# Second block, attention: the relative bias comes from a skewed table and is added to the mask on GpSimd, not by a matmul on TensorE

## The reference, cut to what matters

```
q, k, v, qi, ki, wi = jnp.split(h @ w_in, A_SPLITS, axis=-1)
score = jnp.einsum('bth,bths->bts', wib, relu(qi . ki * IDX_DIM ** -0.5))
score = jnp.where(causal, score, -jnp.inf)
_, idx = lax.top_k(score, top_k)                  # top_k = 64
bias = rel_table[rel_bucket(q_pos - idx)]         # one value per head and distance
logits = q . k[idx] * scale + bias
p = jax.nn.softmax(jnp.where(valid, logits, -jnp.inf), axis=-1)
o = p @ v[idx];   out = o @ w_out
```

## Time and profile before

| | |
|---|---|
| median of 3 runs | 1785.63 us (1784.55 to 1786.57) |
| the profiled execution, its own time | 1787.35 us |
| its span in the profile | 1785.6 us |
| TensorE busy | 1611.1 us, 90% |
| VectorE, ScalarE, GpSimd busy | 898.4, 722.1, 168.2 us |
| mean granted TensorE clock | 0.946 of full speed |

### The profile page before, as it was taken

The page is one execution under the profiler, slowest core; times in us unless marked ns, Lnnn a source line. Parts: engine busy times, 40 slices in busy tenths (PEclk is TensorE's granted clock), DMA queues, the critical chain, the costliest instruction groups (busy, mean ns, idle before and its releaser), DMA issues.

```text
span 1785.6 us, 26627 instructions
## 1 busy us (share of the span) xinstructions
PE 1611.1 (90%) x11038; PEld 1328.8 (74%) x11038; DVE 898.4 (50%) x1104; ACT 722.1 (40%) x936; POOL 168.2 (9%) x82
## 2 busy tenths in 40 slices
PE   6999985767676689999998999999999999999998
PEld 4877742323232358999997999989999899998886
DVE  4765210101010158566585765686656657566665
ACT  4434220101010155445335544464445665355443
POOL 0200000000000002111001111111111001111110
PEclk9999897878787889999899999999999999999999
DMA  9568999999999986555541555556555555455551
GB/s 366 182 231 315 406 427 427 427 429 428 429 427 428 426 294 198 189 183 174 179 156 65 187 184 188 181 189 204 186 190 193 197 183 172 151 183 179 196 186 62
DMA packets 181648, 446.18 MB, mean 250 GB/s; under 512 B 8022, under 2 KB 139471, under 8 KB 163127
## 3 DMA queue, kind: packets, MB, share of 16 engines
q1 hardware_dynamic: 178080, 437.84, 66.3%
q10 hardware_dynamic: 3062, 4.98, 0.8%
q0 software_dynamic: 416, 2.10, 0.3%
HBM read 443.83 MB, written 1.06 MB: 249 GB/s over the span
## 4 chain that ended last, share of the span: by engine, by line
PE 72%; DMA 17%; DVE 6%; ACT 2%; issue 1%; SPq 0%; POOL 0%; DVEq 0%; ACTq 0%
PE wk L838 16%; PE wk L841 8%; DMA arena<-in_w_up_dram 8%; PE wk L1320 8%; PE acc L810 5%; PE acc L811 5%; PE acc L812 5%; DMA ex_ring<-in_w_up_dram 4%; PE wk L810 3%; DMA ring<-in_w_up_dram 3%; PE wk L811 3%; PE wk L812 3%; DVE w_lo L593 2%; PE wk L890 2%; PE wk L891 2%
## 5 line engine op out<-in xcount | busy, mean ns | idle before, releaser
L593 DVE TENSOR_TENSOR w_lo<-ring,w_hi 128x2048 fp32r<-128x2048 f32 x198 | 452.7, 2289 | 189.2 <-ACT w_hi L584 188.5
L584 ACT ACTIVATE w_hi<-ring 128x2048 fp32r<-128x2048 f32 x198 | 377.4, 1907 | 236.1 <-PE acc L812 97.8
L838 PE MATMUL wk<-h_both,w_hi 128*128 128x512 f32 x1344 | 336.9, 392 | 2.3 <-DVE gated L2609 1.3
L838 PEld LDWEIGHTS wk<-h_both,w_hi 128*128 128x128 f32 x1344 | 242.3, 189 | 47.5 <-issue 2.5
L2165 POOL TENSOR_TENSOR hid_lo<-gated,hid_hi 128x512 fp32r<-128x512 f32 x44 | 124.8, 2836 | 1123.5 <-ACT hid_hi L1972 1123.5
L810 PE MATMUL acc<-hid_hi,w_hi 128*128 128x256 f32 x720 | 204.7, 284 | 1.4 <-DVE arena L2825 0.8
L811 PE MATMUL acc<-hid_lo,w_hi 128*128 128x256 f32 x720 | 203.7, 283 | 0.0
L812 PE MATMUL acc<-hid_hi,w_lo 128*128 128x256 f32 x720 | 203.7, 283 | 0.0
L841 PEld LDWEIGHTS wk<-h_both,w_lo 128*128 128x128 f32 x1344 | 183.4, 190 | 13.1
L841 PE MATMUL wk<-h_both,w_lo 128*128 128x256 f32 x1344 | 187.4, 282 | 0.0
L1320 PE MATMUL wk<-ex_ring,arena 128*32 128x512 f32 x400 | 112.3, 750 | 64.6 <-DMA arena<-in_w_up_dram 64.6
(11 more groups left out here) (431 smaller groups left out, 2791.5 us busy)
## 6 DMA issues: line engine op xcount, KB each, us to landing
ring<-in_ffn_w_in_dram SPq DMA_DIRECT2D x88, 1024.0 KB, 5.1
ring<-in_ffn_w_out_dram SPq DMA_DIRECT2D x44, 1024.0 KB, 4.9
ring<-in_w_ada_dram SPq DMA_DIRECT2D x24, 1024.0 KB, 6.7
ring<-in_b_w_in_dram SPq DMA_DIRECT2D x24, 1024.0 KB, 5.2
ex_ring<-in_w_up_dram SPq DMA_DIRECT2D x9, 2048.0 KB, 15.6
ex_ring<-in_w_down_dram SPq DMA_DIRECT2D x9, 2048.0 KB, 24.2
ex_ring<-in_w_gate_dram SPq DMA_DIRECT2D x9, 2048.0 KB, 24.6
ring<-in_w_gate_dram SPq DMA_DIRECT2D x8, 2048.0 KB, 24.4
```

The source lines that it names most:

```text
L584: nc.scalar.activation(w_hi[:, v % SPLIT, 0:n], ring[:, u % RING, 0:n], ACT.Copy).then_inc(w_hi_ready, 1)
L593: eng.tensor_tensor(w_lo[:, v % SPLIT, 0:n], ring[:, u % RING, 0:n], w_hi[:, v % SPLIT, 0:n].bitcast(F32), ALU.subtract).then_inc(w_lo_rea ...
L838: mm(banks[:, m, :], wh[:, k, f], h_both[:, k, :, :], start=k == 0, stop=False, skip_group_check=True)
```

## The change

Four things change, in code written out by hand:

1. `reldist_dram` has 128 copies of each head's row. They are written by one DMA with a broadcast source (8 partitions). It is read back with a partition step of 511 instead of 1, so that row p is shifted by 127 - p: the queries come in the right order and `flip` isn't needed.
2. TensorE's bias matmul (L1548) goes, and with it TensorE's wait for `bias_in`.
3. GpSimd adds bias and mask for each head into `bias_mask` (`masked_bias`), two buffers in the place of `relb`. VectorE's L2764 adds `bias_mask` instead of `amask` and waits for `mask_ready`, one count per head.
4. ScalarE copies the second pair of value banks before it splits unit VA+14.

```diff
-        reldist_dram = nc.dram_tensor("reldist_dram", (HEADS2, 512), F32, kind="Internal").ap()
+        reldist_dram = nc.dram_tensor("reldist_dram", (HEADS2, P, 512), F32, kind="Internal").ap()
...
+        rel_at = used[0]
         relb = area(1024).rearrange("p (b k) -> p b k", b=2)
+        bias_mask = arena[:, rel_at:rel_at + 1024].rearrange("p (b t k) -> p b t k", b=2, t=2)
...
-                if h == 0:
-                    pe.wait_ge(bias_in, 16)
                 for t in range(TT):
-                    o = wk[:, h % 2, t * T:(t + 1) * T]
-                    mm(o, qA[:, h, t * P:(t + 1) * P], kA[:, h, :], start=True, stop=False)
-                    last = mm(o, flip, bias[:, h, P * (1 - t):P * (1 - t) + T], start=False, stop=True)
+                    last = mm(wk[:, h % 2, t * T:(t + 1) * T], qA[:, h, t * P:(t + 1) * P], kA[:, h, :],
+                              start=True, stop=True)
...
-            act.dma_start(reldist_dram, reldist[:, :]).then_inc(reldist_out, 16)
+            act.dma_start(reldist_dram, reldist.rearrange("h (o n) -> h o n", o=1).to_broadcast([HEADS2, P, 512])).then_inc(reldist_out, 16)
...
-            act.dma_start(bias, bass.AP(reldist_dram.tensor, 0, [[1, P], [512, HEADS2], [1, 384]])).then_inc(bias_in, 16)
+            act.dma_start(bias, bass.AP(reldist_dram.tensor, P - 1, [[511, P], [P * 512, HEADS2], [1, 384]])).then_inc(bias_in, 16)
...
             split_high(VA + 11)
+            split_high(VA + 12)
             for pair in range(2):
-                split_high(VA + 12 + 2 * pair)
                 for t in range(TT):
                     A(vA[:, t, pair * 512:(pair + 1) * 512], bank(U_A + 12 + 2 * pair), ACT.Copy,
                       scale=rstd[:, T + t:T + t + 1]).then_inc(grp_out, 1)
-                if pair == 0:
-                    split_high(VA + 13)
+                split_high(VA + 13 + pair)
...
+            def masked_bias(h):
+
+                if h >= 2:
+                    pool.wait_ge(a_max, h - 1)
+                for t in range(TT):
+                    last = nc.gpsimd.tensor_tensor(bias_mask[:, h % 2, t, :], bias[:, h, P * (1 - t):P * (1 - t) + T],
+                                                   amask[:, t, :], ALU.add)
+                last.then_inc(mask_ready, 1)
+            pool.wait_ge(bias_in, 16)
+            pool.wait_ge(mask_ready, 1)
+            masked_bias(0)
+            masked_bias(1)
             for h in range(HEADS2):
+                if h + 2 < HEADS2:
+                    masked_bias(h + 2)
                 pool.wait_ge(apv_ready, h + 1)
                 low(mix_lo[:, h, :], mixA[:, h, :], mix_hi[:, h, :], mix_lo_ready)
...
-            dve.wait_ge(mask_ready, 1)
...
-                link(V.tensor_tensor(lgA[:, h % 2, :, :], wk[:, h % 2, :].rearrange("p (t k) -> p t k", t=2), amask,
-                                     ALU.add))
+                dve.wait_ge(mask_ready, h + 2)
+                link(V.tensor_tensor(lgA[:, h % 2, :, :], wk[:, h % 2, :].rearrange("p (t k) -> p t k", t=2),
+                                     bias_mask[:, h % 2, :, :], ALU.add))
```

## The result

| | kernel before | changed kernel |
|---|---|---|
| median | 1786.1 us (1784.55 to 1788.67, 4 runs) | 1824.95 us (1823.68 to 1827.67, 4 runs) |
| ratio, 95% interval | | 1.0218 [1.0206, 1.023] |
| span of the profiled execution | 1785.6 us | 1825.9 us |
| mean granted TensorE clock | 0.946 | 0.936 |

The account below looks back on a forecast made before the run. The attention of eight heads was taken as bound by TensorE. Ring 19.6 + value banks 0.2 + clock 5.5 = 25.3 us, table write 0, on the median of 1785.63: 1810.9 us, range 1803 to 1822.

Parts of the forecast that it names:

- Part 1: Attention heads: without the bias matmuls TensorE needs 2.16 us a head, and heads would follow about 2.3 us apart.
- Part 2: GpSimd's adds of bias and mask: their order makes heads 3 to 7 take 6.88 us each against 3.03, +19.6 us.
- the ring: Heads 3 to 7: GpSimd's adds, VectorE, TensorE, ScalarE and GpSimd's subtraction wait in a circle, 6.88 us per head.
- Part 3: Value banks copied first, before head 0: scores start 1.9 us sooner, but VectorE's w_lo moves later, +0.2 us.
- Part 4: TensorE in the attention: rests of 4.5 us per turn let its clock fall to half, 0 to 11.5 us, 5.5 taken.
- Part 5: Bias table's 2 MB write at 64 us: taken as 0, at most 10 us if it delays modulation loads.
- a late write: Table write still running beyond 96 us, delaying modulation weight loads with little slack: 1 to 10 us.
- B: Rival: the ring and also a late write, adding 1 to 10 us, 1812 to 1826, middle 1815; chance 0.26.
- a spread write: Table write at 64 us, spread like any 1.5 MB transfer: over by about 75 us, cost 0.
- C: Rival: GpSimd's adds don't bind, heads 3 to 7 fall to VectorE's 2.33 us and save 3.5 us, 1782; chance 0.04.

Follow-up runs that it names:

- the half write: Kernel before with only the early broadcast write of the bias table, 64 copies instead of 128: 1793.08 us, ratio 1.0034.
- the run with the adds ahead: Changed kernel with GpSimd's additions of head h+4, instead of h+2, in front of the subtraction of head h: 1799.94 us, ratio 1.0077 to the kernel before.

## Why the prediction was right or wrong

- **Part 1, the matmuls that go**: the mechanism held. Without them VectorE sets the pace, at 2.40 us a head on average (2.25 and 2.56) instead of the 2.3 I gave, and the prize is 4 us.
- **Part 2, the ring**: right, down to the size. At full clock a turn is 6.89 to 6.91 us against 6.88; reordering GpSimd's list alone removes it, and 25 us with it, the clock's part among them. That head 2 stays outside the ring was right too. So 19.6 of the loss were foreseen as they came.
- **Part 3, the value banks**: predicted +0.2, no difference measured; the add of head 0 is 0.1 to 0.2 us later, as worked out. The gain of 1.7 us at the scores doesn't reach the end.
- **Part 4, the clock**: the mechanism was right and the size too small. I took 5.5 as the middle of 0 to 11.5; the runs give 8.4. From head 2 to head 7 it was 41.29 - 5 x 6.88 = 6.9 us, since all five turns ran at half speed, the first one too, where besides the scores of head 3 stand in front of the ring's transposes. Behind head 7 it was 1.5 instead of up to 3.3 (the terms I named for that bound, 1.30 and one more value pair of 0.86, add up to 2.2 only; the 3.3 isn't worked out), and the output projection cost 0 instead of 3.0. What failed is the reason for the middle ("the clock may come back between"): it does come back, but behind the ring's work of the turn, and it is gone before the next transposes, so that it shortens none of the ring's steps.
- **Part 5, the table**: this is the step that failed. "I take 0" was 12 us. I weighed one load, issued at 95.96, with 1.4 us of slack. But the load that was hit is the one issued at 76.52, in the middle of the write, whose slack I hadn't looked up: before, it was in use 7.0 us after its issue, 0.3 us of slack by the 6.7 us that I reckoned with. The bound failed as well. I let a load be late by no more than its own 6.7 us. Beside this write the load took 20.3 us, some 13 us too long, with some 30 us of the write left at its issue; beside the half write it was 6.8 us late, with some 8 left. In both it was late by no more than the rest of the write; the first delay is twice the bound that I had set. My reason against a late write ("only one or two loads have so little slack") counted the loads and not the size of one delay. The figure of the Trainium skill for a narrow source ("SBUF — State Buffer", section "Door 1: The DMA port swizzle"), 39 us by my estimate from it, was close to the 40 measured.
- **The rivals**: B, the ring and a late write, is what happened, near the end of its 1812 to 1826 and 10 us above its middle. Its chance of 0.26 was too low: the row of the write showed 8 partitions for 2 MB, and the case for a spread write had no row at all. C needed another order, and even with that order no kernel came below the one before by what can be measured.

Sum by what was measured, against the span: 12.0 (write) + 0.2 (value banks) + 19.6 (ring) + 8.4 (clock) = 40.2, of 40.3. That it meets within 0.1 is partly luck: the part up to head 0 varies between executions by more than that. With the same early write, head 0's add starts at 956.96 in the changed kernel and at 952.51 in the run with the adds ahead.

Left open: why the load issued at 76.52 landed when it did. That its delay grows with the write is shown; how the two queues share the engines is not. That eight partitions, and not SBUF as such, make the write slow was tried by no run with a wider source. A narrow write of all 2 MB at a time when no load is tight was not tried.

## What to carry to other kernels

Before a helper engine is put between two steps, write its list in order and follow each wait to the step that it stands behind: two additions behind one late subtraction made 3.03 us a head into 6.9, and the same work in another order cost nothing of that. A DMA out of a few partitions can be slow for its whole length (here 49 to 52 GB/s out of eight) and hold a load of another queue, so look at every load that is issued while it runs, and let the write's remaining time, not the load's own, be the upper bound of its delay. First measure the prize with the work left out (here 4 us) and compare it with what the change adds.

## What the runs showed that I had not expected

- A write from 8 partitions moves at 49 to 52 GB/s, and a 1 MB load of another queue beside it is in use 20.3 us after its issue instead of 7.0; with half the bytes 13.8.
- The granted clock went back to 1.00 at the end of three of the ring's bursts, stayed there while TensorE rested, and was 0.50 again before the next burst began.
- Seven useless matmuls behind the scores of heads 4 to 7 make the changed kernel 4.6 us shorter by the spans and 2.8 us by the medians.
- VectorE's pair of 128x256 TENSOR_SCALARs takes 1.54 us beside GpSimd's additions and 0.61 without them, while its add from a PSUM bank keeps its 0.68 us.
